# Two parity banks, a new order of products and accumulating transfers in a Strassen-like FFN stage

## The reference

```python
def swiglu(h, w_in, w_out):
    g, u = jnp.split(h @ w_in, 2, axis=-1)
    return (jax.nn.silu(g) * u) @ w_out
```

## Time and profile before

| | us |
|---|---|
| median of 3 runs | 1668.2 |
| lowest, highest | 1667.28, 1673.39 |
| profiled execution | 1674.29 |
| its span | 1672.2 |
| PE busy | 1627.2 (97%) |
| DVE busy | 1197.2 (72%) |
| ACT busy | 637.5 (38%) |
| POOL busy | 192.0 (11%) |
| mean granted clock of TensorE, share of full | 0.984 |

### The profile page before, as it was taken

How to read it: one execution, slowest core, us unless ns; L and a number is a source line. 1 busy time by engine, 2 the same in 40 slices (tenths; PEclk the granted TensorE clock), 3 DMA queues, 4 the chain that set the end, 5 groups by cost and what they waited for, 6 DMA issues and landing times.

```text
span 1672.2 us, 25029 instructions
## 1 busy us (share of the span) xinstructions
PE 1627.2 (97%) x9342; PEld 1419.2 (85%) x9342; DVE 1197.2 (72%) x1961; ACT 637.5 (38%) x898; POOL 192.0 (11%) x136
## 2 busy tenths in 40 slices
PE   9999999999998999999999999987998999999998
PEld 6788888889876998888888988887888998999997
DVE  5877777777588687777777883766455687666665
ACT  3321222224788432212222332243323357544443
POOL 0000000000796000000000000333033003000000
PEclk7999999999999999999999999999998999999999
DMA  8755555542201155555554252464354322155552
GB/s 313 280 201 183 186 196 188 205 151 98 102 30 73 51 185 217 185 185 195 188 206 171 101 202 101 113 163 125 110 132 123 126 102 76 52 183 195 188 201 76
DMA packets 57159, 257.47 MB, mean 154 GB/s; under 512 B 6272, under 2 KB 6400, under 8 KB 38656
## 3 DMA queue, kind: packets, MB, share of 16 engines
q1 hardware_dynamic: 53056, 249.18, 41.9%
q0 software_dynamic: 4032, 7.34, 2.7%
HBM read 248.11 MB, written 1.05 MB: 149 GB/s over the span
## 4 chain that ended last, share of the span: by engine, by line
PE 83%; DVE 6%; issue 4%; ACT 3%; POOL 3%; DMA 0%; ACTq 0%; DVEq 0%; SPq 0%; POOLq 0%
PE ps L1997 10%; PE ps L2161 10%; PE ps L2162 10%; PE ps L2168 10%; PE ps L1998 10%; PE ps L1999 10%; PE ps L2197 6%; PE ps L2726 5%; PE ps L2024 4%; PE ps L2732 2%; POOL spare L670 2%; PE ps L2345 1%; ACT w_hi L817 1%; PE ps L2257 1%; DVE work L1492 1%
## 5 line engine op out<-in xcount | busy, mean ns | idle before, releaser
L2161 PE MATMUL ps<-a_hi,w_hi 128*128 128x512 f32 x736 | 286.7, 389 | 0.8 <-ACT w_hi L905 0.8
L2162 PE MATMUL ps<-a_lo,w_hi 128*128 128x512 f32 x736 | 286.4, 389 | 0.0
L1434 DVE TENSOR_TENSOR w_lo<-raw,w_hi 128x2048 fp32r<-128x2048 f32 x98 | 224.1, 2287 | 28.8 <-ACT w_hi L862 13.5
L1997 PE MATMUL ps<-h_hi,w_lo 128*128 128x512 f32 (+1 forms) x648 | 235.3, 363 | 0.3 <-DVE w_lo L1434 0.2
L1998 PE MATMUL ps<-h_lo,w_hi 128*128 128x512 f32 (+1 forms) x648 | 233.5, 360 | 0.0
L1999 PE MATMUL ps<-h_hi,w_hi 128*128 128x512 f32 (+1 forms) x648 | 233.5, 360 | 0.0
L2168 PE MATMUL ps<-a_hi,w_lo 128*128 128x512 f32 x736 | 174.3, 389 | 0.0
L2161 PEld LDWEIGHTS ps<-a_hi,w_hi 128*128 128x128 f32 x736 | 138.1, 188 | 30.2 <-issue 0.8
L2162 PEld LDWEIGHTS ps<-a_lo,w_hi 128*128 128x128 f32 x736 | 138.2, 188 | 28.7
L2168 PEld LDWEIGHTS ps<-a_hi,w_lo 128*128 128x128 f32 x736 | 138.1, 188 | 28.7
L1240 DVE CUSTOM_DVE_ANT_0 mring<-mring,cb 128x1024 f32<-128x1024 f32 x128 | 156.1, 1220 | 0.0
(11 more groups left out here) (395 smaller groups left out, 3225.8 us busy)
## 6 DMA issues: line engine op xcount, KB each, us to landing
raw<-wstream SPq DMA_DIRECT2D x132, 1024.0 KB, 5.3
mring<-wmod SPq DMA_DIRECT2D x144, 512.0 KB, 3.5
spare<-wstream SPq DMA_DIRECT2D x11, 1024.0 KB, 4.8
extra<-wstream SPq DMA_DIRECT2D x28, 256.0 KB, 3.3
raw<-wstream SPq DMA_DIRECT2D x14, 512.0 KB, 5.5
raw<-wstream SPq DMA_DIRECT2D x14, 256.0 KB, 4.6
extra<-extra POOLq DMA_DIRECT2D x14, 256.0 KB, 3.4
raw<-raw POOLq DMA_DIRECT2D x14, 256.0 KB, 4.3
```

The lines of the kernel that those rows point to most:

```text
L1434: dve.tensor_tensor(w_lo[:, slot], raw[:, slot], w_hi[:, slot].bitcast(F32), ALU.subtract).then_inc(lo_ready, 1)
L1997: pe.matmul(dst, lhs_lo, rhs_hi, start=start, stop=False, skip_group_check=True)
L2161: pe.matmul(bank, hi, a_hi[:, k, 0:nt], start=k == 0, stop=False, skip_group_check=True)
L2162: pe.matmul(bank, hi, a_lo[:, k, 0:nt], start=False, stop=False, skip_group_check=True)
```

## The change

Five things change, all in the seven-product slabs.

1. Banks: product 3 is now the one with token sum 0 and goes to the second gate bank, which alternates by parity (2 or 7); product 4 is the one with token sum 3 and goes to an up bank, 5 or 6 by parity. The odd bank is written once a slab. `PLACE` says at which column block of the ring each product finds its weights.
2. TensorE's waits: none before product 3 and 4 except, in odd slabs, for the output banks' evictions; before product 6 it waits for the third combination. A stage starts when both halves of an earlier output slab are evicted.
3. VectorE's order: `neg_u2` first, the splits of parts 0 and 1 together after `neg_u3`, the split of part 3 after the multiply. ScalarE's order: the second Silu before the copy of part 3. In the last slab of a stage the plain slab's copy waits for product 4 (fifth signal) and not for the fourth.
4. Weight sums: all four by accumulating transfers that GpSimd issues: s3 and s1, then s2 from s3, then s4 from s2. For this up-upper and gate-upper are loaded a second time, into the places of s2 and s4.
5. Loads: four transfers with seven quarters in place of five, in larger contiguous pieces (three, two, one and one quarter).

```diff
+PLACE = (0, 1, 2, 4, 3, 5, 6)
...
-        GATE1_BANK, GATE2_BANK, ODD_BANK, MID_BANK = (0, 1), 2, 3, 4
+        GATE1_BANK, GATE2_BANK, ODD_BANK, MID_BANK, UP_BANK = (0, 1), (2, 7), 3, 4, (5, 6)
...
-                sp.dma_start(extra[:, p, 2 * QUARTER:3 * QUARTER], block(2)).then_inc(fast_loaded[p], 16)
-                sp.dma_start(extra[:, p, QUARTER:2 * QUARTER], block(3)).then_inc(fast_loaded[p], 16)
-                sp.dma_start(raw[:, p, QUARTER:2 * QUARTER], block(3)).then_inc(fast_loaded[p], 16)
-                sp.dma_start(raw[:, p].rearrange("p (a n) -> p a n", n=QUARTER)[:, 0::2],
-                             wstream[ds(w, 1), :, 0:2 * QUARTER].rearrange("a p (b n) -> p (a b) n", b=2)) \
-                  .then_inc(raw_loaded[p], 16)
+                sp.dma_start(extra[:, p], blocks(0, 3)).then_inc(fast_loaded[p], 16)
+                sp.dma_start(raw[:, p, 0:2 * QUARTER], blocks(0, 2)).then_inc(raw_loaded[p], 16)
+                sp.dma_start(raw[:, p, 2 * QUARTER:3 * QUARTER], blocks(3, 4)).then_inc(fast_loaded[p], 16)
+                sp.dma_start(raw[:, p, 3 * QUARTER:SLAB], blocks(3, 4)).then_inc(fast_loaded[p], 16)
...
+                a22, s1, a12, s4 = (raw[:, p, c * QUARTER:(c + 1) * QUARTER] for c in range(4))
+                s2, s3, a11 = (extra[:, p, c * QUARTER:(c + 1) * QUARTER] for c in range(3))
+                pool.dma_start(s3, a11, accum_op=ALU.add).then_inc(col_added, 16)
+                pool.dma_start(s1, a22, accum_op=ALU.add).then_inc(row_added[p], 16)
                 pool.wait_ge(col_added, 16 * (n + 1))
-                pool.tensor_tensor(extra[:, p, 0:QUARTER], extra[:, p, QUARTER:2 * QUARTER], raw[:, p, 0:QUARTER],
-                                   ALU.add).then_inc(three_added, 1)
-                pool.wait_ge(three_added, n + 1)
-                pool.tensor_tensor(raw[:, p, 3 * QUARTER:SLAB], extra[:, p, 0:QUARTER],
-                                   raw[:, p, 2 * QUARTER:3 * QUARTER], ALU.add).then_inc(four_added, 1)
+                pool.dma_start(s2, s3, accum_op=ALU.add).then_inc(three_added, 16)
+                pool.wait_ge(three_added, 16 * (n + 1))
+                pool.dma_start(s4, s2, accum_op=ALU.add).then_inc(four_added[p], 16)
...
                 else:
-                    act.wait_ge(prod_done, N_PROD * n + 4)
+                    act.wait_ge(prod_done, N_PROD * n + 5)
                     split_hi(w + 1, (w + 1) % 2, w + 1)
                 act.wait_ge(prod_done, value_at(i, N_PROD, N_PROD * n + 6))
                 act.activation(sil[:, p, 0:LAT], ps[GATE1_BANK[p]][:, 0:LAT], ACT.Silu)
+                act.wait_ge(combined, value_at(i, N_COMB, N_COMB * n + 5))
+                act.activation(sil[:, p, LAT:TOK], gate2, ACT.Silu).then_inc(sil_ready, 1)
                 act.wait_ge(slab_done, value_at(i, 1, w + 1))
...
-                if ahead:
-                    part_low(0, n + 1, w + 1, 1 - p, i)
                 product(2)
...
                 if ahead:
+                    part_low(0, n + 1, w + 1, 1 - p, i)
                     part_low(1, n + 1, w + 1, 1 - p, i)
                 product(4)
                 earlier(2)
-                dve.tensor_tensor(up_sum[:, 0:LAT], neg_u3, ps[ODD_BANK][:, 0:LAT], ALU.subtract).then_inc(combined, 1)
+                dve.tensor_tensor(up_sum[:, LAT:TOK], neg_u3, ps[GATE2_BANK[p]][:, 0:LAT],
+                                  ALU.subtract).then_inc(combined, 1)
                 product(5)
...
+                if ahead:
+                    part_low(3, n + 1, w + 1, 1 - p, i)
...
-                comb(1)
-                product(3, odd, sum_part(3), True, True)
-                pe.wait_ge(pair_free, i + (f + 2))
-                product(4, gate2_bank, sum_part(0), True, False)
+                if p:
+                    for t in range(2):
+                        pe.wait_ge(out_free[t], b + 2)
+                product(3, gate2_bank, sum_part(0), True, False)
+                product(4, up, sum_part(3), True, True)
                 pe.wait_ge(first_copied, i + (n + 1))
                 product(5, gate1, plain_part(1, 0), False, True)
-                comb(4)
+                pe.wait_ge(combined, i * N_COMB + (N_COMB * n + 3))
                 product(6, gate2_bank, plain_part(1, 1), False, True)
```

More of the change, by code:

```diff
@@ L337, in build @@
         three_added = sem("three_added")
-        four_added = sem("four_added")
+        four_added = [sem(f"four_added{i}") for i in range(2)]
         part_hi = sem("part_hi")
@@ L591, in quarter_loads, with blocks @@
             def quarter_loads(w, p, wait):
-                def block(c):
-                    return wstream[ds(w, 1), :, c * QUARTER:(c + 1) * QUARTER].rearrange("a p n -> p (a n)")
+                def blocks(c0, c1):
+                    return wstream[ds(w, 1), :, c0 * QUARTER:c1 * QUARTER].rearrange("a p n -> p (a n)")
                 sp.wait_ge(lo_ready, wait)
-                sp.dma_start(extra[:, p, 2 * QUARTER:3 * QUARTER], block(2)).then_inc(fast_loaded[p], 16)
-                sp.dma_start(extra[:, p, QUARTER:2 * QUARTER], block(3)).then_inc(fast_loaded[p], 16)
-                sp.dma_start(raw[:, p, QUARTER:2 * QUARTER], block(3)).then_inc(fast_loaded[p], 16)
-                sp.dma_start(raw[:, p].rearrange("p (a n) -> p a n", n=QUARTER)[:, 0::2],
-                             wstream[ds(w, 1), :, 0:2 * QUARTER].rearrange("a p (b n) -> p (a b) n", b=2)) \
-                  .then_inc(raw_loaded[p], 16)
+                sp.dma_start(extra[:, p], blocks(0, 3)).then_inc(fast_loaded[p], 16)
+                sp.dma_start(raw[:, p, 0:2 * QUARTER], blocks(0, 2)).then_inc(raw_loaded[p], 16)
+                sp.dma_start(raw[:, p, 2 * QUARTER:3 * QUARTER], blocks(3, 4)).then_inc(fast_loaded[p], 16)
+                sp.dma_start(raw[:, p, 3 * QUARTER:SLAB], blocks(3, 4)).then_inc(fast_loaded[p], 16)
             def fast_loads(w0, size):
@@ L811, in part_high @@
                 if part == 1:
-                    act.wait_ge(three_added, value_at(i, 1, n + 1))
+                    act.wait_ge(three_added, value_at(i, 16, 16 * (n + 1)))
                 if part == 2:
@@ L815, in part_high @@
                 if part == 3:
-                    act.wait_ge(four_added, value_at(i, 1, n + 1))
+                    act.wait_ge(four_added[p], value_at(i, 8, 16 * (n // 2 + 1)))
                 act.activation(ring_hi[:, RING[part]], part_source(part, p), ACT.Copy) \
@@ L840, in fast_step @@
                     split_hi(w + 2, w % 2, w + 2)
-                act.wait_ge(combined, value_at(i, N_COMB, N_COMB * n + 5))
-                act.activation(sil[:, p, LAT:TOK], gate2, ACT.Silu).then_inc(sil_ready, 1)
                 act.wait_ge(pair_free, value_at(i, 1, f + 3))
@@ L1486, in fast_step @@
                 dve.wait_ge(slab_done, value_at(i, 1, w + 1))
-                dve.tensor_tensor(gate2, ps[GATE2_BANK][:, 0:LAT], neg_u2, ALU.subtract).then_inc(combined, 1)
-                if ahead:
-                    part_low(3, n + 1, w + 1, 1 - p, i)
+                dve.tensor_tensor(gate2, ps[GATE2_BANK[p]][:, 0:LAT], neg_u2, ALU.subtract).then_inc(combined, 1)
                 dve.wait_ge(sil_ready, value_at(i, 1, f + 1))
@@ L2170, in plain_slab, with fast_slab @@
                 last.then_inc(slab_done, 1)
-            def fast_slab(w, f, n, i):
+            def fast_slab(w, f, n, b, i):
                 p = n % 2
-                gate1, gate2_bank, odd, mid = (ps[c][:, 0:LAT] for c in (GATE1_BANK[p], GATE2_BANK, ODD_BANK, MID_BANK))
+                gate1, gate2_bank, odd, mid, up = (ps[c][:, 0:LAT] for c in (GATE1_BANK[p], GATE2_BANK[p], ODD_BANK,
+                                                                             MID_BANK, UP_BANK[p]))
                 def plain_part(kk, b):
@@ L2181, in sum_part @@
                     return lambda x, k: x[1][:, c, k]
-                def comb(k):
-                    pe.wait_ge(combined, i * N_COMB + (N_COMB * n + k))
                 def product(r, bank, moving, start, end):
@@ L2194, in product @@
                         for k in range(4):
-                            c0 = r * QUARTER + k * P
+                            c0 = PLACE[r] * QUARTER + k * P
                             for x in ((a_hi, t_hi), (a_lo, t_lo)) if high else ((a_hi, t_hi),):
@@ L2220, in ffn @@
                     if g in FAST[s]:
-                        pe.wait_ge(out_free[0], b + 1)
+                        for t in range(2):
+                            pe.wait_ge(out_free[t], b + 1)
                         if g == FAST[s][0]:
@@ L2225, in ffn @@
                             for j in range(2):
-                                fast_slab(w + j, f + j, FAST_BASE[s, g] + j, i)
+                                fast_slab(w + j, f + j, FAST_BASE[s, g] + j, b, i)
                     else:
@@ L2807, in _ffn_slabs @@
         if g in fast:
-            part = part.reshape(size, P, 4, QUARTER)[:, :, (3, 1, 0, 2)].reshape(size, P, SLAB)
```

(1 more changed line is left out.)

7 lines of the change are left out of this document (1 added, 6 removed).

## The result

| us | before | after |
|---|---|---|
| median of 4 runs | 1668.92 | 1689.01 |
| lowest, highest | 1667.28, 1673.39 | 1688.81, 1691.37 |
| profiled execution | 1674.29 | 1688.81 |
| its span | 1672.2 | 1686.8 |

The ratio is 1.0119 (95% interval 1.0097 to 1.0141). The forecast was 1660.8 with a range of 1645 to 1676.

The account below looks back on a forecast made before the run. TensorE was taken as the bound, with 40.1 us recoverable in two stages. Stages 12.4 us under 181.5, less 5 of half clock, gave -7.4: 1668.2 to 1660.8 us, range 1645 to 1676.

Parts of the forecast that it names:

- The stall in front of product 3: TensorE's wait, once a slab, for the subtraction that frees the odd bank: 24.1 us, all freed by the new banks.
- a loop over two slabs: Loads, s3, s2, then part 1's copy and split and the third subtraction hold up product 6: P = 25.05 us.
- the s2 link under the loads: Second of two chained sums, s3 then s2: 6.9 us undisturbed, 7.7 taken, with only one under the loads.
- Its upper bound for the two links together: s3 and s2 with one landing slowed by loads from 4.3 to 6.8 us: 9.4 us.
- 169.05 + 5: Both seven-product stages after the change, 97.05 and 72.0 us, plus 5 us taken for half clock.
- links of 5 us: Sign in the profile after: if the summing transfers' links take 5 us, contention is under-priced.
- The half clock: Products at TensorE's lower clock after gaps: 15.8 us today, 5 taken; only a slow product 6 counts.
- 5P + 43.8: Time of both seven-product stages without the clock term, P being the length of the loop over two slabs.
- The DMA work: The sixteen engines' transfers per slab go from 7.0 to 11.7 us, above TensorE's 10.1.
- the hidden case: Rival: undisturbed links and quick loads give P = 21.9, stages 28.2 us less, 1640 us; chance 0.20.
- The stall at each stage's end: The plain slab's copy waits for one product more in each stage's last slab: 1.6 to 1.7 us a stage.
- The slower rival: Contention in the sixteen DMA engines gives P = 27.95 and 8 us of half clock: +10, 1678 us; chance 0.16.

Follow-up runs that it names:

- experiment 1: The changed kernel with the loads and weight sums of the kernel before (five quarters, two additions on GpSimd): 1640.88 us, 0.9839 of before.
- experiment 11: The changed kernel with a slab's loads issued only once the previous slab's s3 transfer has landed: 1690.03 us, 1.0096 of before.
- experiment 4: The changed kernel without loading the two gate-upper blocks: five quarters, four transfers kept, results not valid: 1675.3 us, 1.0038 of before.
- experiment 10: The changed kernel with a slab's loads issued only after the previous slab's s2 transfer has landed: 1707.96 us in one execution.
- (3): The changed kernel with its seven quarters loaded by seven transfers of 256 KB instead of four larger ones: 1691.93 us, 1.0145 of before.
- 9: Before's weight sums with changed banks and queues, products 3 and 4 swapped back, five quarters in three loads instead of four: 1635.33 us, 0.9799 of before.

## Why the prediction was wrong

**The stall in front of product 3 goes: right.** No wait on the first combination is left, and experiment 1 shows what it was worth once the transfers are out: 27 us of the median (1668.1 to 1640.9 on one chip), 27 of the stages.

**It moves to product 6, by way of the s2 transfer and a loop over two slabs: right**, in every step and in the place (in the first pair the s3 transfer takes the larger share of the delay). The mechanism was the forecast's; one term was mis-sized. Slab 2 to slab 4 is 1144.67 - 1114.04 = 30.6 us against the 25.05 forecast:

| step | forecast | measured |
|---|---|---|
| slab start to load issue | 3.45 | 3.5 |
| loads, to the first sum | 9.7 | 9.8 |
| s3 | 3.45 | 3.65 |
| s2 | 4.25 | 8.25 |
| copy, split, subtraction, product 6 | 4.2 | 5.4 |

**The step that failed is the price of the s2 link under the loads.** The prediction had a row of a disturbed landing, 2.5 us above the median, and took less than a third of it. Its upper bound for the two links together was 9.4; they took 11.9. Of the 22.8 us by which the stages exceed the forecast's 169.05 + 5, the s2 term gives 5 x 4.0 = 20. The s2 link beside seven quarters is 8.5 to 8.7 us in experiment 11 and 5.6 to 9.9 in the changed kernel, 7.6 to 9.3 beside five (4), and 3.6 beside none (10). So the row that was at hand, one s1 landing of 6.8 us in the kernel before, was near to what five quarters do (7.4 for slab 4 of experiment 4), and it was read as the rare case when it was the normal one of the new rhythm. The prediction's own sign for this, links of 5 us, is what the trace shows.

**The half clock** was put at 5 us over both stages. Only product 6 counts, as forecast, but it does in every pair: 2.72 us instead of 1.44, 1.3 us five times, 6.4 us. With 30.6 us a pair, which has this in it, the forecast's own sum, 5P + 43.8, gives 196.8 us; the profile has 196.8.

**The DMA work** of 11.7 us a slab was used as an argument against the hidden case, and that case is out. **The stall at each stage's end**, 1.6 to 1.7 us forecast, is 3.1 us over two stages. **The slower rival** had the mechanism and the right sign; by its rule P = 30.6 is far past its point of decision of 28.2. It was given 0.16 because the disturbed links were held to be few.

The prediction also misread a row: 4.3 us is not the best landing of a sum but that of s1, which is issued 0.6 us behind s3; the page of the kernel before has 3.4 for s3 (extra<-extra). It did not enter the sum, which went by the link of 3.45.

By the rule of the Trainium skill that the prediction cites (DMA: Bandwidth & Descriptors, "Anatomy of one DMA — SWDGE (gpsimd) path"), a 256 KB transfer is estimated at 2.6 us. The runs show 3.3 for the landing at best and 8.2 beside a slab's loads, so the measurement decides. By the Trainium skill (DMA: Bandwidth & Descriptors, "Queues, rings and completion order") the DMA engines take turns between queues; this fits the direction but does not by itself give the size.

What stays open is why a sum of 256 KB, about 1.6 us of the engines' work, lasts nearly as long as the loads beside it. It is the loads that do it (10), not the size of their pieces (3), nor the 2.2 us by which it stood behind them (11), and two quarters less of them take off only 0.8 us (4). The s1 transfer just ahead of it in GpSimd's queue is not enough: it is there in experiment 10 too. Whether accumulating from SBUF to SBUF or the GpSimd queue is at fault was not tried, nor was a sum issued well ahead of the loads.

## What to carry to other kernels

The transfer that replaced some 1.5 us of an engine cost 3.6 us alone and up to 9.9 beside loads; price each link of a chain of dependent transfers by its time under load, and count the links and the bytes that the change itself adds. Where a change makes two kinds of transfer meet in every turn that met seldom before, the rare slow row of the old trace can become the typical one of the new, as here. When a change has two halves, sum each by itself: here the banks and queues alone were worth 27 us, 33 with larger loads and the old order of products, and the seven quarters and four transfers cost 48 on top of them (23 in the kernel before). The gain of the one half is lost while the loop of the other sets the pace.

## What the runs showed of the hardware

- A summing transfer of 256 KB inside SBUF: landed in 3.3 us, a link of 3.6, with no load beside it (experiment 10); links of 5.6 to 9.9 us beside a slab's loads of 1.8 MB (the changed kernel), 7.6 to 9.3 beside 1.3 MB (4). The s2 transfer of slab 4 landed within 0.5 us of the last of the loads beside it.
- After each of its five waits of 8.5 to 9.0 us in front of product 6, the changed kernel's TensorE was at the lower of its two levels of the granted clock: the next product took 2.72 us instead of 1.44. In experiment 4 waits of 4.7 to 6.2 us did the same. In the kernels with no long waits (1, 9) the clock of these stages was 1.00 throughout.
- Two executions of the kernel before differed by 5 us in these stages by half clock alone (granted clock 0.93 and 0.89, 0.95 and 0.95), at nearly the same idle time.
